# Delta rule: blocks of the upper row half turned by the transpose instruction instead of a product with the unit matrix

## What is computed

```
lower = where(strict, (kb @ kc.T) * decay, 0)
t_inv = triangular_solve(eye + lower, eye)       # inverse of a unit lower triangle
u = t_inv @ vb;  w = t_inv @ (kb * exp(gc))
v_new = u - w @ s;  o = qg @ s + intra @ v_new;  s = s * g_last + kg.T @ v_new
```

## Time and profile before

| | us |
|---|---|
| median of 3 runs | 1643.85 (1643.5 to 1644.07) |
| profiled execution, time | 1640.94 |
| profiled execution, span of the trace | 1638.9 |
| mean granted TensorE clock | 0.921 of full speed |
| PE busy in the span | 1413.3 (86%) |
| DVE / ACT / POOL busy | 649.2 / 550.2 / 179.4 |

### The profile page before, as it was taken

How to read it: one execution, slowest core, us unless ns; L and a number is a source line. 1 busy time by engine, 2 the same in 40 slices (tenths; PEclk the granted TensorE clock), 3 DMA queues, 4 the chain that set the end, 5 groups by cost and what they waited for, 6 DMA issues and landing times. The chain is left out here.

```text
span 1638.9 us, 25689 instructions
## 1 busy us (share of the span) xinstructions
PE 1413.3 (86%) x10025; PEld 993.3 (61%) x10026; DVE 649.2 (40%) x1030; ACT 550.2 (34%) x1067; POOL 179.4 (11%) x160
## 2 busy tenths in 40 slices
PE   4998999689999889888997989989964799998950
PEld 2444999555578677776886987768824333333310
DVE  3332463357711223445763103347634223222317
ACT  1123234168721633434212214341110333433324
POOL 0000000014300031210000000000000122221215
PEclk9999999789988978999998999999985899999985
DMA  9111111133002220003104116433260488895335
GB/s 322 58 39 40 39 52 51 37 91 117 1 27 81 90 103 15 3 3 123 54 39 141 39 52 257 180 109 141 83 276 34 153 265 273 268 311 183 78 65 223
DMA packets 83685, 185.03 MB, mean 113 GB/s; under 512 B 12948, under 2 KB 48923, under 8 KB 77171
## 3 DMA queue, kind: packets, MB, share of 16 engines
q1 hardware_dynamic: 76523, 157.14, 26.9%
q0 software_dynamic: 6912, 25.17, 6.5%
q10 hardware_dynamic: 144, 1.25, 0.2%
HBM read 144.31 MB, written 39.31 MB: 112 GB/s over the span
## 5 line engine op out<-in xcount | busy, mean ns | idle before, releaser
L3048 PE MATMUL bank<-arena,hT 128*64 x384 | 176.9, 605 | 9.3 <-DVE hT L3164 5.4
L3048 PEld LDWEIGHTS bank<-arena,hT 128*64 128x64 f32 x384 | 51.2, 139 | 110.7 <-issue 107.9
L479 PE MATMUL bank<-arena,hT 128*128 128x512 f32 x256 | 112.4, 597 | 0.0
L2140 PE MATMUL bank<-hT_rest,f_w_high 128*128 128x352 f32 x288 | 93.2, 324 | 0.0
L3051 PE MATMUL bank<-arena,hT 128*64 128x512 f32 x192 | 90.0, 614 | 0.0
L3074 PE MATMUL bank<-arena,hT 128*64 x192 | 87.5, 598 | 0.7 <-ACT hT L3115 0.7
L3051 PE MATMUL bank<-h,hT 128*64 128x512 f32 x192 | 87.0, 595 | 0.0
L479 PEld LDWEIGHTS bank<-arena,hT 128*128 128x128 f32 x256 | 48.6, 192 | 58.1 <-issue 58.0
L3002 POOL DMA_INDIRECT expert_sums<-hT,row_slot x24 | 47.4, 1976 | 220.9 <-DVE hT L3170 177.8
L2139 PE MATMUL bank<-hT_high,q_w_high 128*128 128x352 f32 x192 | 62.7, 326 | 4.0 <-DVE q_w_low L2432 4.0
L2139 PE MATMUL bank<-f_h_high_a,f_w_high 128*128 128x352 f32 x180 | 58.9, 327 | 6.7 <-DVE f_w_low L689 6.7
(11 more groups left out here) (488 smaller groups left out, 3241.6 us busy)
## 6 DMA issues: line engine op xcount, KB each, us to landing
arena<-in_ex_wg_dram SPq DMA_DIRECT2D x16, 1024.0 KB, 4.9
arena<-in_ex_wu_dram SPq DMA_DIRECT2D x16, 1024.0 KB, 8.2
arena<-in_ex_wd_dram SPq DMA_DIRECT2D x16, 1024.0 KB, 12.0
tokens<-h SPq DMA_DIRECT2D x24, 512.0 KB, 2.7
arena<-in_cache_mem_k_dram SPq DMA_DIRECT2D x8, 1024.0 KB, 4.9
arena<-in_w_in_dram SPq DMA_DIRECT2D x12, 512.0 KB, 4.0
h<-tokens SPq DMA_DIRECT2D x6, 1024.0 KB, 7.1
h<-in_x_prompt_dram SPq DMA_DIRECT2D x8, 512.0 KB, 8.8
```

Source lines behind the costliest of these rows:

```text
L479: last = nc.tensor.matmul(ps[bank][0:r, 0:n], hT[:, k, i * P:i * P + r], wt[:, k, col:col + n], start=(k == 0), stop=(k == KC - 1))
L2140: nc.tensor.matmul(out, high, w_low, start=False, stop=False)
L3048: nc.tensor.matmul(ps[UPB[u % 2]][rows_of(0), :], xT[:, u % 2, k, rows_of(0)], gate_up_of[:, bass.ds(slot, 1), :, k, :].rearrange("p a g f ...
```

## The change

A helper `turned(out, block, q, o, m)` turns one block. For a block of the upper row half (o = 0) it issues the transpose instruction with the 64 x 64 corner of the unit matrix, for one of the lower half (o = 64) the product with the unit matrix as before. `level` uses it at level 1, and `transposed` at every level. At level 32 `transposed` turns the upper half only, and ScalarE copies only those 64 partitions. Tile 0 has only an upper block of 32 rows, so all its turns become transpose instructions. Nothing else differs; the order of heads and halves is kept, so the transposes of the upper half and the products of the lower half alternate.

```
+            def turned(out, block, q, o, m):
+                if o == 0:
+                    return nc.tensor.transpose(out, block, K("ident", m, m))
+                return nc.tensor.matmul(out, block, K("ident")[q, o:o + m], start=True, stop=True)
...
                     for h in range(HEADS):
                         for q, o in chunks(j):
-                            rhs = K("ident")[q, o:o + m] if lvl == 1 else Y[q, h, :]
-                            last = nc.tensor.matmul(py(j)[q, h * m:(h + 1) * m], L[q, h, o:o + m], rhs, start=True, stop=True)
+                            out = py(j)[q, h * m:(h + 1) * m]
+                            if lvl > 1:
+                                last = nc.tensor.matmul(out, L[q, h, o:o + m], Y[q, h, :], start=True, stop=True)
+                            else:
+                                last = turned(out, L[q, h, o:o + m], q, o, m)
...
                 for h in range(HEADS):
-                    for q, o in chunks(j):
-                        last = nc.tensor.matmul(ps[5][q, h * m:(h + 1) * m], Y[q, h, :], K("ident")[q, o:o + m], start=True, stop=True)
+                    for q, o in chunks(j)[0:1 if lvl == 32 else 2]:
+                        last = turned(ps[5][q, h * m:(h + 1) * m], Y[q, h, :], q, o, m)
...
                 w = HEADS * hb(j)
-                r = rw(j)
+                r = HB if lvl == 32 else rw(j)
                 nc.scalar.copy(B("X", j)[0:r, 0:w], ps[5][0:r, 0:w]).then_inc(turn_ev, 1)
```

## The result

The changed kernel is slower: 1775.59 us (1765.31 to 1786.46, six runs) against 1643.35 us of the kernel before in the same comparison, a ratio of 1.0822 with a 95% interval of 1.0784 to 1.0859. That is 132 us, where 78 were forecast; the range ended at 1768.

The account below looks back on a forecast made before the run. TensorE's queue, in written order, was taken to bound the stage and so the kernel. Sets +55, low-clock sets +4, level 32 -1 and clock +20 made +78 on the median 1643.85, 1722 us; range 1688 to 1768.

Parts of the forecast that it names:

- What bounds the kernel, and the halves side by side: Stage of the change: TensorE's queue sets its length; upper and lower half products overlap, sixteen passes in 0.46 us.
- A transpose of 64 columns changes the form: In the turned sets: such a transpose stands in full-width mode, so alternating with lower-half products changes form and prevents overlap.
- no change of form: Rival for the sets: transposes keep the products' form, sets stay at 0.46 us, time the same; chance 0.05.
- passes count: Rival: halves don't overlap, 300 passes saved at 0.03 to 0.058 us, 9 to 17 us faster, 1630; chance 0.03.
- cheap changes: Rival: a transpose's edges overlap with weight loads, a head costs half, +29 us without a clock fall, 1673; chance 0.06.
- Sets: 48 sets with both halves, level 1 and below level 32: 1.61 against 0.46 us each, +55 us (48 to 70).
- the entry edge: Start of a turned set: its first transpose pays 0.11 us for the change of form unless TensorE has just idled.
- Level 32 and tile 0: Level 32: four transposes replace eight sets' products, 0.37 against 0.46 us, -0.7 us, ScalarE's copy unchanged; tile 0: 0.
- The clock: Stage of the change: sparser matmuls leave TensorE's granted clock at 0.50 for longer, +20 us.
- 50 us more at 0.50: Stage of the change: 50 us more at half the granted clock, each losing 0.39 us, +20 us.
- The bounds of that step: Extra time at half clock: none of the stage (0) or all of it (+130 us or more).
- clock falls for most of the stage: Rival: +58 us plus 0.39 of some 250 us lost at half clock, 1800 us; chance 0.08.

Follow-up runs that it names:

- products by half: The kernel before, no transposes; in 48 sets the four upper-half products come first, then the four lower-half ones: 1653.29 us, ratio 1.0076.
- grouped: The changed kernel with each set's four upper-half transposes first and its four lower-half products behind them: 1681.7 us, ratio 1.0238.
- wide version: The changed kernel with products of 128-column weights (64*128) in place of upper-half transposes, in three of four heads, all four at level 1: 1814.69 us, ratio 1.1051.
- thick version: The kernel before plus three unread 64-column products per half ahead of each head's pair in 48 sets: 1704.38 us, ratio 1.0395.
- level-32 product version: The kernel before with only the upper half turned and copied at level 32, still as a product: 1643.16 us, ratio 1.0036.
- thin: The kernel before plus three unread 4-column products per half ahead of each head's pair in 48 sets: 1790.88 us, ratio 1.0896.

## Why the prediction was right and wrong

**What bounds the kernel, and the halves side by side: right.** The waits of the stage turned as the prediction said (VectorE and ScalarE wait longer, their busy time is unchanged, TensorE's own waits stay), and products by half, which take the overlap away, cost 13 us without any transpose.

**A transpose of 64 columns changes the form: right.** The rivals "no change of form" (only level 32 gains, 1642), "passes count" (1630) and "cheap changes" (1673) fall with the head of 0.43 us; 0.42 to 0.48 was worked out. With no product between them four transposes take 779.26 - 778.95 = 0.31. What is shown is the cost of the alternation, by the grouped and the wide version; that a transpose of 64 columns stands in a full-width mode remains the prediction's reading of the earlier trace rows; no run shows it directly. Fewer passes were no gain here: the stage has 2915 matmuls in place of 3215, and the ratio is 1.0822.

**Sets: right, +1.07 us each where 1.15 was taken.** 48 x 1.07 = 51 us against 55. The thick version prices nearly the same length on its own, heads of 0.47 us for +64 us. The 1.07 is of a set after a pause; one right behind `update` has 0.10 ahead of it, the entry edge that the prediction put at 0.11. If half the sets had it in full, 48 sets would make 54 us.

**Level 32 and tile 0: right.** 0.32 us for the four transposes, forecast 0.37; no measurable gain. ScalarE's copy of 64 partitions and 256 columns took 365 ns (L1957 of the changed kernel, x8), that of 128 partitions 372 (x40), so it kept its time as the prediction had it.

**The clock: the step that failed.** The prediction's term "50 us more at 0.50", +20 us, had the right direction and the wrong size: it was 215 - 38 = 177 us more in the stage, worth 58 to 80 us, or 69 at the prediction's own 0.39. 51 and 58 to 80 make 109 to 131, and the stage grew by 117. With 177 in place of 50 the sum would have been 1641 + 58 + 177 x 0.39 = 1768 for the profiled execution, which took 1766; that it comes so close is in part luck, since the sum has 55 for the sets and nothing for the 8 us outside the stage. The bounds of that step, none of the stage or all of it, held the answer, but the range took only 0 to +55 us from it. The value of 50 was drawn from the stretches of before, though the sets after would be unlike them: the count worked out there (24 matmuls in over 3 us, under half of a round at 1.00) pointed the other way, and so did, where the clock stands at 0.50 behind a row of products with 4 columns. The rival "clock falls for most of the stage", with a chance of 0.08, is what happened: 215 of 307 us were at 0.50. Its price doesn't agree with the step before it, 0.39 of 250 us in one place and +130 or more in the other.

**Not in the sum:** 8 us outside the stage. They are the clock too: the mean of 0.870 over the span makes 2 x 0.130 x 1764.2 = 459 us at 0.50, 244 of them outside the stage against 221 before, and 23 x 0.39 is 9. The level-32 product version has 19 more there without being slower in the stage, so this doesn't need the change of the sets.

**The spread of the six executions** is mostly the clock as well. The shortest (1765.31 us, span 1763.5, mean clock 0.872) has 451 us at 0.50, the longest (1786.46, span 1784.7, 0.861) 496; 45 us at 0.33 to 0.45 are 15 to 20 of the 21 us between them. The profiled execution is one of the shorter ones, so the clock's part in the median is, if anything, larger than reckoned here.

**What stays open.** That in the change the empty time around each change of form thins the sets is an inference from the thin and thick versions, which change no form, and from the grouped one, where fewer changes go with less time at 0.50; no run has changes of form and dense sets at once. By count the changed set is the thinner of the two: a head has three passes of 64 columns in 0.43 us, one of the thin version twelve of 4 and four of 64 in 0.47. A part played by the transpose as such isn't excluded either, since the grouped transposes had more time at 0.50 than the products by half. When within the stage the clock rises again isn't explained, nor what makes one execution spend more time at 0.50 than another.

## What to carry to other kernels

In this case small products of the two row halves ran side by side while they alternated and kept the same form (0.46 us for a set of sixteen passes between runs of that form; where the set took 0.61 us, by half it took 0.86); a transpose, or a product with weights 128 columns wide, between them ended that (0.43 and 0.62 us a head in place of 0.115), and the smaller count of passes, 12 in place of 16, said nothing of it. If transposes are wanted, keep those of one form together, as in the sets of level 32 (no cost) or the grouped version (+2.4% in place of +8.2%). And when an edit makes a long stretch of TensorE's queue thinner, cost the clock over the whole stretch as the likely case and not as an edge of the range: here it went from 38 to 215 us at 0.50 and was about half of the loss, or more.

## What was not expected of the hardware

- The granted clock fell to 0.50 for 239 of 342 us in a stage in which TensorE shows as busy 93% of the time and 2304 of its 5520 matmuls (48 sets of 48) had 4 columns; with 64 columns in those it was 15 of 248 us.
- A wide product (64*128) between 64*64 products cost more than a transpose in the same place: 0.62 against 0.43 us a head at clock 1.00.
- A head with two changes of form lost a third at half clock (0.43 to 0.64 us, where twice would be 0.86), less than the 0.45 of the plain products of L1728 (1.07 to 1.94): part of its time did not double with the halved clock.
